# Three output-projection tiles begun inside the attention loop, two blocks of rotations finished later, and value matmuls grouped by pairs

## The reference

```
o = gate_c * softmax(q k_cmp) v_cmp + gate_s * softmax(q k_s) v_s + gate_w * softmax(q k_w) v_w   # 16 heads of 64
h = h + (o * silu(z)) @ w_out                 # output projection of the attention, 1024 x 1024
u, z = split(rmsnorm(h) @ w_in)               # second mixer
x[t] = a * x[t-1] + (b u)[t]                  # 64 groups x 64 complex states, a scan over the positions
y = gelu(c x + d u); ... h = h + (...) @ w_out
```

## Time and profile before

| what | us |
|---|---|
| median of 3 runs (1859.52 to 1864.2) | 1859.71 |
| the profiled execution, its own time | 1856.59 |
| its span, first to last instruction | 1854.7 |
| last stretch of the attention without z tiles | 284 to 390.8 |
| output projection | 390.8 to 438.5 |

### The profile page before, as it was taken

One profiled execution on the slowest core, in us unless ns is written; L12 is line 12 of the kernel. 1 busy time (PEld: TensorE's weight loads), 2 busy tenths in 40 slices (PEclk: granted clock), 3 DMA queues, 4 the chain that ended last, 5 costly groups with the idle time before them and its releaser, 6 DMA issues.

```text
span 1854.7 us, 24520 instructions
## 1 busy us (share of the span) xinstructions
PE 1784.1 (96%) x9954; PEld 1455.8 (78%) x9954; DVE 975.3 (53%) x1680; ACT 864.8 (47%) x1486; POOL 164.9 (9%) x293
## 2 busy tenths in 40 slices
PE   5899998899999999999999999999999999999997
PEld 4677886679988877876877777888788878888886
DVE  7878556954764365345345545355544544434223
ACT  6355666645454244246345554266633643223223
POOL 2000226510000000000000000022200011111000
PEclk9899999999999999999999999999999999999999
DMA  3563441035423323311322223222132223322332
GB/s 132 159 213 122 132 115 58 1 100 212 151 95 102 103 80 115 101 57 48 111 90 80 69 70 101 94 69 63 55 108 94 92 69 100 102 94 88 105 94 65
DMA packets 61471, 181.30 MB, mean 98 GB/s; under 512 B 7136, under 2 KB 20256, under 8 KB 58928
## 3 DMA queue, kind: packets, MB, share of 16 engines
q1 hardware_dynamic: 61360, 179.75, 29.9%
HBM read 165.57 MB, written 16.25 MB: 98 GB/s over the span
## 4 chain that ended last, share of the span: by engine, by line
PE 82%; DVE 10%; ACT 5%; issue 1%; POOL 1%; DMA 0%; SPq 0%; DVEq 0%; ACTq 0%
PE bank L1002 19%; PE bank L1004 19%; PE bank L1003 18%; PE bank L1096 2%; PE bank L1097 2%; PE bank L1098 2%; PE bank L1259 2%; DVE wlo L2116 1%; PE bank L1238 1%; ACT L1525 1%; PE bank L1022 1%; PE bank L1023 1%; PE bank L1024 1%; PE bank L1228 1%; PE bank L1118 1%
## 5 line engine op out<-in xcount | busy, mean ns | idle before, releaser
L2116 DVE TENSOR_TENSOR wlo<-wraw,whi 128x1024 fp32r<-128x1024 f32 (+1 forms) x262 | 316.4, 1210 | 276.4 <-ACT whi L1520 275.2
L1002 PE MATMUL bank<-Hh,whi 128*128 128x512 f32 (+2 forms) x1104 | 442.9, 401 | 12.2 <-DVE wlo L2116 12.2
L1004 PE MATMUL bank<-Hh,wlo 128*128 128x512 f32 (+2 forms) x1104 | 432.4, 392 | 0.0
L1003 PE MATMUL bank<-Hl,whi 128*128 128x512 f32 (+2 forms) x1104 | 432.1, 391 | 0.0
L1520 ACT ACTIVATE whi<-wraw 128x1024 fp32r<-128x1024 f32 (+1 forms) x262 | 271.9, 1041 | 297.5 <-PE bank L1004 227.6
L1002 PEld LDWEIGHTS bank<-Hh,whi 128*128 128x128 f32 (+2 forms) x1104 | 206.9, 187 | 69.2 <-DVE wlo L2116 14.1
L1004 PEld LDWEIGHTS bank<-Hh,wlo 128*128 128x128 f32 (+2 forms) x1104 | 207.0, 188 | 45.9
L1003 PEld LDWEIGHTS bank<-Hl,whi 128*128 128x128 f32 (+2 forms) x1104 | 207.1, 188 | 44.8 <-issue 1.7
L1525 ACT ACT_TABLE_LOAD x102 | 130.9, 1283 | 2.9 <-DVE epst L2141 1.1
L2889 POOL TENSOR_SCALAR bs<-dist 128x256 f32<-128x256 f32 x16 | 7.4, 460 | 796.7 <-DMA dist<-in_c_dist 795.9
L1002 PE MATMUL bank<-Bh,whi 128*128 128x512 f32 x192 | 75.8, 395 | 0.0
(11 more groups left out here) (393 smaller groups left out, 3230.7 us busy)
## 6 DMA issues: line engine op xcount, KB each, us to landing
wraw<-in_w_o SPq DMA_DIRECT2D x24, 512.0 KB, 3.5
wraw<-in_w_bgate SPq DMA_DIRECT2D x24, 512.0 KB, 3.5
wraw<-in_w_branch SPq DMA_DIRECT2D x24, 512.0 KB, 3.4
wraw<-in_w_fg SPq DMA_DIRECT2D x22, 512.0 KB, 3.5
wraw<-in_w_fu SPq DMA_DIRECT2D x22, 512.0 KB, 3.5
wraw<-in_w_glu SPq DMA_DIRECT2D x16, 512.0 KB, 3.5
wraw<-in_w_fd SPq DMA_DIRECT2D x16, 512.0 KB, 3.5
scratch_CA<-CA SPq DMA_DIRECT2D x4, 1152.0 KB, 6.6
```

What stands on the lines that cost most here:

```text
L1002: pe.matmul(o, wh[:, cols], hi(k), start=k == 0, stop=False)
L1003: pe.matmul(o, wh[:, cols], lo(k), start=False, stop=False)
L1004: m = pe.matmul(o, wl[:, cols], hi(k), start=False, stop=k == K - 1)
L2116: dve.tensor_tensor(c.wlo[q][:, 0:n], c.raw[i % RR][:, 0:n], c.whi[q][:, 0:n].bitcast(F32), S_).then_inc(*up(DID, ("wlo", i)))
```

## The change

Three edits. First, `part_of` does some contraction steps of a projection tile, and tiles 0, 1 and 2 are begun inside the attention loop at i = 57, 64, 67, 68, 69 and 70 (first contraction step, last one excluded: `AHEAD`); behind the loop each has only its contraction step 7 left. The `pair` is gone. Second, the value group of j = 0 is no longer done at i = 8t + 7 but together with that of j = 1, at i = 8t + 9. Third, columns 32 to 64 of state blocks 2 and 3 are no longer made in the attention: the copy to `Rt` takes blocks 0 and 1 whole and columns 0 to 32 of blocks 2 and 3, and VectorE makes the rest in `Rt` in the second mixer, after `a0` (step `R2`).

```
         self.attention()
-        self.pair([("w_o0", 0), ("w_o0", 1)], "g0")
         for t in range(8):
-            if t >= 2:
+            if t < 3:
+                self.part_of("w_o0", t, KT - 1, KT)
+            else:
                 self.gemm("w_o0", t, "g0")
             self.evict(("w_o0", t))
...
+    def part_of(self, w, col, k0, k1, src="g0"):
+
+        key = (w, col)
+        if k0 == 0:
+            self.tiles[key] = (src, KT, 128)
+            self.bank.take(key)
+            self.begun[key] = self.piece(w, (col,), 0, KT * 128)
+        self.step("mm", key, self.begun[key], 0, k0, k1, k1 == KT)
+
+
+    AHEAD = {57: (0, 0, 4), 64: (1, 0, 4), 67: (0, 4, 7), 68: (1, 4, 7), 69: (2, 0, 4), 70: (2, 4, 7)}
...
             if i % 3 != 2:
                 self.tick()
+            if i in (57, 64):
+                self.part_of("w_o0", *self.AHEAD[i])
             if i % 2 == 0 and 2 <= i <= n:
                 self.step("nb", i - 2)
             if 4 <= i <= n + 3:
                 stage_c(i - 4)
-            if i % 2 and i >= 7:
+            if i in (67, 68):
+                self.part_of("w_o0", *self.AHEAD[i])
+            if i % 2 and i >= 7 and units[i - 7][2]:
+                if units[i - 7][2] == 1:
+                    stage_d(i - 9)
                 stage_d(i - 7)
+            if i in (69, 70):
+                self.part_of("w_o0", *self.AHEAD[i])
...
-            if i in range(AWAY + 10, AWAY + 28):
+            if i in range(AWAY + 10, AWAY + 22):
                 self.step("prep_r_wide", *divmod(i - AWAY - 10, 6))
...
-        order = ("a0 b0 m1 a1 e0 b1 r0 a2 ...
+        order = ("a0 R2 b0 m1 a1 e0 b1 r0 a2 ...
...
         w, b0, b1 = [(16, 0, 4), (32, 0, 2), (32, 2, 4)][part]
+        r = c.Rh if part < 2 else c.Rt
...
+        flat = [x[:, :] for x in c.tR] if part < 2 else [x[:, :, :].rearrange("p q n -> p (q n)") for x in (c.xt, c.wre)]
+        t1, t2 = [x.rearrange("p (b q n) -> p b q n", q=8, n=w) for x in flat]
...
+        if part == 2:
+            on.wait_ge(*at("Rt"))
...
             on.wait_ge(*at("pv", 63, 1))
-            sp.dma_start(c.Rt[:, :, :, :, :].rearrange("p b i q n -> p (b i q n)"),
-                         c.Rh[:, :, :, :, :].rearrange("p b i q n -> p (b i q n)")).then_inc(*land("in_R", ("Rt",)))
+            sp.dma_start(c.Rt[:, 0:2, :, :, :].rearrange("p b i q n -> p (b i q n)"),
+                         c.Rh[:, 0:2, :, :, :].rearrange("p b i q n -> p (b i q n)")).then_inc(*land("in_R"))
+            sp.dma_start(c.Rt[:, 2:4, :, :, 0:32].rearrange("p b i q n -> p (b i q) n"),
+                         c.Rh[:, 2:4, :, :, 0:32].rearrange("p b i q n -> p (b i q) n")).then_inc(*land("in_R", ("Rt",)))
```

More of the change, by code:

```diff
@@ L118, in __init__ @@
         self.own = {}
+        self.begun = {}
         self.nsa()
@@ L637, in fetch_m, with rotations @@
             self.step("fetch_m", b)
-        fns = dict(a=first_half, b=other_half, e=norm_turned, r=rows, s=states, o=outputs, t=turned, z=z_tile, y=split_y,
+        def rotations(part):
+            for n in range(6):
+                self.step("prep_r_wide", part, n)
+        fns = dict(R=rotations, a=first_half, b=other_half, e=norm_turned, r=rows, s=states, o=outputs, t=turned, z=z_tile, y=split_y,
                    w=fetch_w, m=fetch_m)
-        order = ("a0 b0 m1 a1 e0 b1 r0 a2 s0 w2 b2 r1 a3 s1 w3 r2 b3 o0 m2 s2 z0 r3 t0 o1 m3 z1 s3 y0 t1 z2 o2 y1 z3 t2 "
+        order = ("a0 R2 b0 m1 a1 e0 b1 r0 a2 s0 w2 b2 r1 a3 s1 w3 r2 b3 o0 m2 s2 z0 r3 t0 o1 m3 z1 s3 y0 t1 z2 o2 y1 z3 t2 "
                  "o3 y2 z4 t3 y3 z5 z6 z7")
@@ L2248, in prep_r_wide @@
         w, b0, b1 = [(16, 0, 4), (32, 0, 2), (32, 2, 4)][part]
-        R = lambda i, n0, n1: c.Rh[:, b0:b1, i, :, n0:n1]
-        last = lambda i: c.Rh[:, b0:b1, i, :, w - 1:w].broadcast_to([128, b1 - b0, 8, w])
-        t1, t2 = [x[:, :].rearrange("p (b q n) -> p b q n", q=8, n=w) for x in c.tR]
+        r = c.Rh if part < 2 else c.Rt
+        R = lambda i, n0, n1: r[:, b0:b1, i, :, n0:n1]
+        last = lambda i: r[:, b0:b1, i, :, w - 1:w].broadcast_to([128, b1 - b0, 8, w])
+        flat = [x[:, :] for x in c.tR] if part < 2 else [x[:, :, :].rearrange("p q n -> p (q n)") for x in (c.xt, c.wre)]
+        t1, t2 = [x.rearrange("p (b q n) -> p b q n", q=8, n=w) for x in flat]
         on.wait_ge(*at("Rs"))
+        if part == 2:
+            on.wait_ge(*at("Rt"))
         if n in (0, 3):
@@ L2257, in prep_r_wide @@
         else:
-            tt(R(n // 5, w, 2 * w), t1, t2, A_ if n == 5 else S_, *([("Rh",)] if (part, n) == (2, 5) else []))
+            tt(R(n // 5, w, 2 * w), t1, t2, A_ if n == 5 else S_, *([("Rh",)] if (part, n) == (1, 5) else []))
     def nb(u):
```

## The result

The changed kernel takes **1866.58 us** (median of 7 runs, 1864.78 to 1867.18). The kernel before, run beside it, takes 1860.15 (7 runs, 1859.17 to 1864.2). The ratio is 1.0027, with a 95% interval of 1.0016 to 1.0039. In a later comparison the two stood at 1866.54 and 1862.73, ratio 1.0020 (1.0012 to 1.0029). So the change makes the kernel 4 to 6 us slower. The forecast of 1869 is 2.4 us above the time. As a difference, +9.7, it is too large by 3.3 to 5.9 us: most runs of the kernel before are above the 1859.7 from which it started. The profiled executions differ by more, 1866.58 against 1856.59; why is told under "The sum against the total".

The account below looks back on a forecast made before the run. PE, busy for 96% of the span, was taken to bound the kernel. Attention +7.0 and the chain behind it +2.7 gave +9.7 on 1859.7, so 1869 us; range 1861 to 1878, the main case's own 1864 to 1875.

Parts of the forecast that it names:

- Part 1: Attention, periods without z tiles: moving the j = 0 value group two iterations back costs 0.7 to 0.8 us each, +2.0 taken.
- the 1 us or more named as a sign: Attention: PE's gap ahead of the transposes of i = 41 and 49 would grow by at least this much.
- Part 2: Attention from i = 57: projection matmuls placed there delay the j = 1 group by 1.9 us and add 3.1 after it.
- The bank argument: At i = 57: tile 0's first half needs the bank the transposes wait for, so it starts at about 362.5, not before.
- End of the last value group: End of attention: comes 7.0 us later (2.0 + 1.9 + 3.1), bounds +3 and +12.
- Part 3: Projection: too little PE work covers the chain; PE idles 14.5 us and resumes 21.4 after the last value group, +2.7.
- the copy: Table copy to Rt ahead of the first Hh: taken as 10 us, bounds 7.4 and 19.
- The half-speed stretch behind the gap: Projection, after PE's long idle: loses 1.7 us, as it did before the change.
- Part 4: Second mixer: six rotation instructions, 4.3 us on VectorE, fit a gap of 7.86 us and cost 0; up to 4.3 otherwise.
- Slow rows: Rival on the table copy: short rows make Rt land at 19 us, total 1878 us; chance 0.12.
- Chain and attention cost little: Rival: moved value group free, fill at i = 57 absorbed, Rt landed by 7.4, total 1863 us; chance 0.16.
- Faster: Rival: joined value groups and projection work keep PE running, the 0.87 waits go, -5.8, total 1854 us; chance 0.12.

Follow-up runs that it names:

- joined groups alone: Kernel before with only the value groups of j = 0 and j = 1 done together; 1859.46 us, ratio 0.9991.
- own groups: Changed kernel with each value group back in its own iteration, as before the change; 1864.94 us, ratio 1.0018 to the kernel before.
- begun projection alone: Kernel before with only projection tiles 0, 1 and 2 begun in the attention, whole table copied; 1866.56 us, ratio 1.0029.
- rotations alone: Kernel before with only six rotation steps moved to the second mixer and the shorter copy in two parts; 1859.30 us, ratio 0.9986.
- the kernel with the longer gap of 13.66: Changed kernel with the half of Rt's copy in 4096 rows of 128 bytes moved twice; 1872.91 us, one run.
- joined groups again: Repeat of the kernel before with only the two value groups joined; 1859.71 us, ratio 0.9988.
- own groups with the early split: Changed kernel with separate value groups and weight splits of tiles 3 to 5 emitted behind tiles 0 to 2; 1853.07 us, repeated 1854.64.
- the early split: Changed kernel with weight splits of tiles 3, 4, 5 emitted right behind tiles 0, 1, 2; 1857.41 us, ratio 0.9977 to the kernel before.

## Why the prediction was right or wrong

**Part 1, the group of j = 0 moved behind VectorE's wait.** Forecast +2.0, for i = 41 and 49; the group of i = 57 is a term of part 2. A mark between the parts is VectorE's product with z for head pair 5 (at 359.85 before, 363.53 here). Counted from the first score matmul it comes at 160.0 and 159.6 us in the two profiles before, at 163.7 and 160.4 in the two of the changed kernel: +3.9 in one, +0.6 in the other. The forecast lies between, and its mechanism is not what the traces show. The 0.87 waits are gone, but the wait in front of the transposes of i = 49 grew from 1.79 to 2.15, not by the 1 us or more named as a sign. I had charged the matmuls that come to stand behind the wait at 0.7 to 0.8 us a period. With joined groups alone idle time grows by 0.6 in all, and at full clock the stretch does not grow. What costs is the term I had allowed 0.5 us for (one more half-speed stretch of 1.7, perhaps): 5.1 us more lost on average with joined groups alone, and 8.5 and 5.1 in the changed kernel against 5.1 and 3.4. One trace could not tell its size: the two executions of the changed kernel have nearly the same waits, and differ by 3.4 us lost at half speed and by 3.3 us of attention.

**Part 2, the filling at i = 57 and later.** Forecast 1.9 + 3.1 = 5.0, of which 1.6 is the moved group of i = 57; the gain from the rotations is in it. From the mark to the last value matmul the kernel before takes 30.8 and 31.2 us, the changed one 36.5 both times: +5.5. With own groups it takes 35.2 (three profiles), +4.2, where the forecast without the moved group is 3.4; begun projection alone 35.9, rotations alone 30.0. Right in size, and by its own terms: the wait of 2.07 ahead of 383.08 and the half-speed stretch behind it are gone in all kernels with begun tiles. The bank argument is right too: the first filler matmul is released by VectorE's L2266, as the transposes were. The wait ahead of it is 0.17 us with own groups and 1.43 with joined ones.

**End of the last value group.** +7.0 forecast; +9.4 and +6.1 measured, the difference being that of part 1.

**Part 3, the chain.** Its mechanism is confirmed step by step. `Hh` is released by the DMA of `Rt`; the low weights of tile 3 stand behind three X; 10.8 us from `Hh` to PE's resume against 11.2 forecast. What failed is one term: the copy. I took 10 us out of bounds of 7.4 and 19; it landed 7.3 us after the last value group, at the lower bound. So PE resumed 18.1 us behind it, 0.6 sooner than before (18.7) and not 2.7 later, and the gap is 11.0 instead of 14.5. Half a megabyte in 4096 rows of 128 bytes costs 2.65 us when added. That is what the bounds were missing: the forecast had no row on it. The Trainium skill, "DMA: Bandwidth & Descriptors", says in "Why small descriptors are slow (HBM only)" that transfers inside SBUF don't suffer from short rows; the trace agrees as far as the landing goes (7.2 us; 8 was the estimate by it, 12 the one by the Trainium skill's table in "Specifications"), but not in the rate: the last section has the short rows at 217 GB/s and the whole ones at 354.

**The half-speed stretch behind the gap** I left at 1.7 us. It is 2.9, +1.2. In the kernel with the longer gap of 13.66 it is shorter again (7 matmuls at half speed instead of 13), so its length doesn't follow the gap's. It is also why the projection stretch of that kernel grew by 1.5 and not 2.7.

**Part 4, six rotation instructions in the second mixer.** Forecast 0. They run from 453.8 to 458.1, and PE is at 100% over them:

```profile
453.80:458.20 4.40, 4.40 (x39) 4.40 (x38) 4.22 (x7) 2.35 (x2) 0.00 (x0) 1.00 0.39 119
```

**The sum against the total.** Attention and projection together are 9.9 us longer in the first pair of profiles and 6.4 in the second; the medians differ by 6.4 and 3.8. That 1869 came within 2.4 us of the time is in part luck: a difference that was too large stood on a start that was too low, attention was 2.4 above or 0.9 below its term, and the projection is +0.5 and +0.3 where 2.7 were forecast. The remaining 2.6 to 3.5 us, and the whole of what joined groups alone cost (2.0 to 2.6 over both stretches, nothing or less in the total), lie in the rest. It has nearly the same code in all kernels and still spans 1616 to 1624 us. The two executions of the kernel before show what differs there, first in the 90 us around the second mixer's end (270 to 360 us behind its start; PE's busy time, granted clock):

```profile
708.50:798.50 90.00, 88.25 (x387) 1.00 0.33 106
```

```profile
710.70:800.70 90.00, 88.40 (x377) 0.96 0.33 105
```

The idle is nearly the same, and the clock is 1.00 in the one and 0.96 in the other. Over the whole part behind the second mixer's start it accounts for everything. In all profiles PE has the same four waits of more than 1 us there (1.84, 1.32, 3.01 and 1.58 in the kernel before), and behind them the clock goes to half in some executions and not in others. Behind the 1.84, for instance, the granted clock over 6 us is 1.00 in the first profile of before (from 677.8) and 0.72 in the second (from 680). Where PE lost no busy time at half speed, the part is 1416.3 or 1416.4 us long (four profiles: before, changed, joined groups again, own groups with the early split); with 3.1 to 3.4 us lost 1419.2 to 1419.5 (four); with 4.5 lost 1420.6 (one); with 6.2 to 6.8 lost 1422.1 to 1422.4 (five). The second mixer's rotations don't lengthen it. So a single execution says little about differences below 6 us in the total. The first profile of before, 1616.0, was the shortest rest of all. What is not settled: whether joined groups make short rests likelier (six profiles with them have 1616.1 to 1621.0, mean 1618.2, the eight others 1616.0 to 1624.3, mean 1620.5) or whether that is chance. The medians point the same way: less the kernel's own two stretches and the 1.9 us around the span, they leave 1616 to 1617 for joined groups alone and 1620 to 1622 for the kernel before. No run separates the two.

**The rivals.** Slow rows: fell, the copy landed at 7.2. Chain and attention cost little (1863): its copy term came true, its attention did not. Faster: it needed the wait ahead of the transposes not to grow, and it grew to 2.15. Half of it holds in another form: the changed kernel does give a gain once the next weight splits are freed from the chain, as the early split shows. What the early split would give the kernel before, whose only gap there is 2.07 us, was not run.

## What to carry to other kernels

Work taken out from behind a chain must leave enough to cover it: 42 matmuls (9.7 us) moved ahead left a gap of 11.0, since tile 3's weights were queued behind updates that they don't depend on. Before work is moved, ask what the first instruction after it waits for, and whether that wait is of data or only of queue order. One line that emitted the splits early turned a loss of 4 to 6 us into a gain of 4 to 5 (8 with the value groups left apart). Two short waits gathered into one can cost more than their sum: idle time grew by 0.6 us and the time lost at half speed by 5.1. And where executions of one kernel differ, compare stretches with the half-speed time taken out of them before you price an edit by a trace.

## What the runs showed of the hardware

The DMA rate inside SBUF depends on the row. In the changed kernel from 400 us on, in slices of 0.2 us, the first megabyte (whole rows) goes at a mean of 354 GB/s over 14 slices (the first of them 532, the last 287), then most of the half megabyte in 128-byte rows at an even 216 to 219:

```profile
GB/s 0 0 0 0 0 0 0 532 123 573 328 410 287 369 205 287 410 287 410 451 287 262 130 194 216 219 217 218 216 219 216 216 217 206 255 235 0 164 164 0
```

So short rows do cost: some 5.3 us per MB (2.65 for half a one), where a second megabyte in whole rows adds 3.0 us (5.9 us for 1 MB, 8.9 for 2 MB). In the kernel with the begun projection alone the 2 MB in whole rows take 6.6 us of transfer, 318 GB/s, and land after 9.04 us; 1 MB whole and 1 MB short land after 9.87. It didn't show at landing in the changed kernel because only a quarter of the table, 0.5 MB, went that way, and another quarter was not copied at all.

Behind waits of PE of 1.25 to 2.4 us in a busy stretch the granted clock went to 0.5 in some executions and not in others, with the same code and the same waits: behind the wait of 2.07 at 318 in the first profile of before and not in the second, behind the wait of 1.25 at 363.6 the other way round. The same 90 us of unchanged code ran at a mean granted clock of 1.00 or 0.96.
